# A transformer block pair on one core: the first stage's small work in another order

## The reference

```
xn   = rmsnorm(x, attn_norm_g)
proj = xn @ w_in                    # 1024 x 2312
qa, ka, va, qb, kb, vb, f = split(proj)
qa, ka, qb, kb = rmsnorm of each head (64 wide), with gains
out_a = sliding-window attention (8 query, 2 key heads, alibi, a sink logit per head)
log_f = log_sigmoid(f + b_forget)
out_b = causal attention (8 heads), logit[t, s] += c[t] - c[s], c = cumsum(log_f)
x = x + concat(out_a, out_b) @ w_out
x = x + relu(rmsnorm(x) @ w_up)**2 @ w_down
```

## Time and profile before

| | |
|---|---|
| time, three runs | 1270.38, 1275.14, 1274.62 us; median 1274.62 |
| the profiled execution's own time | 1270.3 us |
| its span, first to last instruction | 1268.4 us |
| TensorE busy | 1208.7 us, 95% of the span |
| VectorE, ScalarE, GpSimd busy | 610.9, 464.6 and 450.8 us |
| mean granted TensorE clock | 0.987 of full |
| first TensorE instruction | 10.12 us |
| tiles 0 to 3 of the first stage (first matmul of tile 0 to first of tile 4) | 14.99 to 48.52 us |
| first scores | 66.40 us |

### The profile page before, as it was taken

One profiled execution on the slowest core, in us unless ns is written; L12 is line 12 of the kernel. 1 busy time (PEld: TensorE's weight loads), 2 busy tenths in 40 slices (PEclk: granted clock), 3 DMA queues, 4 the chain that ended last, 5 costly groups with the idle time before them and its releaser, 6 DMA issues.

```text
span 1268.4 us, 16854 instructions
## 1 busy us (share of the span) xinstructions
PE 1208.7 (95%) x6252; PEld 998.0 (79%) x6252; DVE 610.9 (48%) x907; ACT 464.6 (37%) x828; POOL 450.8 (36%) x188
## 2 busy tenths in 40 slices
PE   5799999998999999999899999999899999999997
PEld 4677877787788788788779887778788888888885
DVE  5555445658767768651657223884721111111115
ACT  5455433425324334234342111432463251341441
POOL 3422220204444453463336320400255435353440
PEclk9999999999999999999889999999999999999999
DMA  7422120206665766643424311202243324233211
GB/s 228 116 85 67 62 87 2 85 17 216 233 215 191 241 211 210 227 134 132 133 67 143 99 67 26 67 2 83 67 140 108 119 67 132 67 105 94 83 50 66
DMA packets 75562, 144.10 MB, mean 114 GB/s; under 512 B 7234, under 2 KB 10050, under 8 KB 75490
## 3 DMA queue, kind: packets, MB, share of 16 engines
q1 hardware_dynamic: 53730, 98.46, 24.7%
q10 hardware_dynamic: 21760, 44.67, 10.6%
HBM read 140.20 MB, written 2.13 MB: 112 GB/s over the span
## 4 chain that ended last, share of the span: by engine, by line
PE 54%; issue 22%; DVE 11%; POOL 8%; ACT 2%; DMA 1%; ACTq 0%; POOLq 0%; DVEq 0%
PE gemm L950 16%; PE gemm L952 16%; PE gemm L951 16%; POOL w_lo L513 8%; DVE nmax L1860 1%; PE aux L1404 1%; DVE prob_t L1674 1%; DVE gemm L1859 1%; PE aux L991 1%; DVE xr L1465 1%; DVE xr L1460 1%; ACT junk L576 1%; DVE xt_lo L1471 1%; DMA mlp_gain<-in_g_pre_mlp 1%; PE gemm L1088 1%
## 5 line engine op out<-in xcount | busy, mean ns | idle before, releaser
L513 POOL TENSOR_TENSOR w_lo<-w_raw,w_hi 128x1024 fp32r<-128x1024 f32 (+1 forms) x180 | 445.7, 2498 | 780.2 <-ACT w_hi L741 422.3
L950 PE MATMUL gemm<-xt_hi,w_hi 128*128 128x512 f32 (+1 forms) x704 | 255.9, 363 | 5.0 <-issue 4.6
L951 PE MATMUL gemm<-xt_lo,w_hi 128*128 128x512 f32 (+1 forms) x704 | 254.8, 362 | 0.0
L952 PE MATMUL gemm<-xt_hi,w_lo 128*128 128x512 f32 (+1 forms) x704 | 254.5, 362 | 0.0
L950 PE MATMUL gemm<-w_hi,ht_hi 128*128 128x512 f32 x512 | 201.4, 393 | 3.8 <-POOL w_lo L513 3.8
L951 PE MATMUL gemm<-w_lo,ht_hi 128*128 128x512 f32 x512 | 200.0, 391 | 0.0
L952 PE MATMUL gemm<-w_hi,ht_lo 128*128 128x512 f32 x512 | 199.7, 390 | 0.0
L741 ACT ACTIVATE w_hi<-w_raw 128x1024 fp32r<-128x1024 f32 x124 | 125.7, 1050 | 175.6 <-PE gemm L952 130.0
L950 PEld LDWEIGHTS gemm<-xt_hi,w_hi 128*128 128x128 f32 x704 | 134.0, 190 | 27.1 <-issue 6.0
L1699 DVE TENSOR_TENSOR ht_lo<-hid,ht_hi 128x512 fp32r<-128x512 f32 x64 | 53.0, 828 | 210.7 <-ACT hid L754 210.7
L951 PEld LDWEIGHTS gemm<-xt_lo,w_hi 128*128 128x128 f32 x704 | 133.9, 190 | 20.2
(11 more groups left out here) (218 smaller groups left out, 1487.0 us busy)
## 6 DMA issues: line engine op xcount, KB each, us to landing
wm<-in_w_mod ACTq DMA_DIRECT2D x64, 512.0 KB, 4.8
w_raw<-in_w_in SPq DMA_DIRECT2D x32, 512.0 KB, 3.8
w_raw<-in_w_up SPq DMA_DIRECT2D x32, 512.0 KB, 4.0
w_raw<-in_w_down SPq DMA_DIRECT2D x32, 512.0 KB, 4.1
w_raw<-in_w_mlp_in SPq DMA_DIRECT2D x32, 512.0 KB, 4.2
w_raw<-in_w_mlp_out SPq DMA_DIRECT2D x32, 512.0 KB, 3.7
w_raw<-in_w_out SPq DMA_DIRECT2D x16, 512.0 KB, 3.7
x<-in_x SPq DMA_DIRECT2D x4, 512.0 KB, 7.7
```

What stands on the lines that cost most here:

```text
L513: pool.tensor_tensor(w_lo[s % 2][:, ks, 0:width], raw[q][:, :, 0:width], w_hi[s % 2][:, ks, 0:width].bitcast(F32), ALU.subtract).then_inc( ...
L950: pe.matmul(bank, lh, rh, start=(k == 0), stop=False)
L951: pe.matmul(bank, lh, rl, start=False, stop=False)
L952: mm = pe.matmul(bank, ll, rh, start=False, stop=(k == KT - 1))
```

## The change

Each engine's program gets another order in the first stage; nothing is computed otherwise.

- ScalarE: slab 0 is rounded in the first two of the four `stat` steps instead of the second and third. The Exp for silu and the copy to negsel leave the place ahead of the head chain, for h = 12 and h = 10.
- TensorE: `turn_heads(g - 3)` instead of `turn_heads(g - 2)` in the middle of tile g, for g = 3 to 7; the last three are at the ends of steps h = 0, 1 and 2. `forget_turns()` moves behind the products of h = 3. `scores(0)` waits for SINK_STEPS = 11 instead of SILU_STEPS = 12 of the same semaphore.
- ScalarE: `head_gain` moves with the turns, to g - 3, and to h = 0, 1 and 2 for tiles 5 to 7.
- VectorE: the sinks' nine instructions move from ahead of the head chain to behind `head_rows(3)`; silu's three to h = 13.

```diff
 # ScalarE
             for m in range(TT):
                 stat(STAT_N1 + m, (x_loaded[m], 16), x[:, m, :])
-                if m in (1, 2):
-                    high_of(0, 2 * m - 2)
-                    high_of(0, 2 * m - 1)
+                if m < 2:
+                    high_of(0, 2 * m)
+                    high_of(0, 2 * m + 1)
                 if m >= 1:
                     xt_high(NT_1 + m - 1, m - 1)
...
-            act.wait_ge(vec_loaded, 16 * 9)
-            did(act.activation(ctmp[:], cvec[:], ACT.Exp, scale=-1.0), silu_act)
-            act.wait_ge(negsel_loaded, 16)
-            did(act.activation(negsel[:], sel_raw[:], ACT.Copy), negsel_ready)
...
-                if g >= 2:
-                    head_gain(g - 2)
+                if g >= 3:
+                    head_gain(g - 3)
...
-                for g in range(6, 16):
-                    if (g - 6 if g < PHASE else tile_end(g) + 3) == h:
+                for g in range(5, 16):
+                    if (g - 5 if g < PHASE else tile_end(g) + 3) == h:
                         head_gain(g)
+                if h == 10:
+                    act.wait_ge(negsel_loaded, 16)
+                    did(act.activation(negsel[:], sel_raw[:], ACT.Copy), negsel_ready)
+                if h == 12:
+                    act.wait_ge(vec_loaded, 16 * 9)
+                    did(act.activation(ctmp[:], cvec[:], ACT.Exp, scale=-1.0), silu_act)
 # TensorE
-                if g >= 2:
-                    if g == 2:
+                if g >= 3:
+                    if g == 3:
                         pe.wait_ge(xt_lo_done, 2 * TT)
-                    turn_heads(g - 2)
+                    turn_heads(g - 3)
...
-                    pe.wait_ge(silu_step, SILU_STEPS)
+                    pe.wait_ge(silu_step, SINK_STEPS)
...
+                for g, k0, k1 in tile_groups(h):
+                    part_product(g, k0, k1)
+                if h < 3:
+                    turn_heads(5 + h)
                 if h == 3:
                     forget_turns()
-                for g, k0, k1 in tile_groups(h):
-                    part_product(g, k0, k1)
-                if h < 2:
-                    turn_heads(6 + h)
 # VectorE
-            (the three instructions of silu and the nine of the sinks, ahead of the gains)
+            def sinks():
+                dve.wait_ge(vec_loaded, 16 * 9)
+                rest = sink
+                for part in range(3):
+                    did(dve.tensor_copy(sink_parts[:, part, :], rest[:]), silu_step)
+                    if part < 2:
+                        did(dve.tensor_tensor(sink_rest[:], rest[:], sink_parts[:, part, :], ALU.subtract), silu_step)
+                    rest = sink_rest
+                did(dve.memset(sink_rows[:], 0.0), silu_step)
+                for part in range(3):
+                    did(dve.tensor_copy(sink_rows[32 * part:32 * part + 1, :], sink_parts[:, part, :]), silu_step)
+            def silu():
+                dve.wait_ge(silu_act, 1)
+                did(dve.tensor_scalar(ctmp[:], ctmp[:], 1.0, None, ALU.add), silu_step)
+                did(dve.reciprocal(csil[:], ctmp[:]), silu_step)
+                did(dve.tensor_tensor(csil[:], csil[:], cvec[:], ALU.mult), silu_step)
             for g in range(PHASE):
                 head_means(g)
                 head_rows(g)
+                if g == 3:
+                    sinks()
...
                 forget_gates(h)
+                if h == 13:
+                    silu()
```

More of the change, by code:

```diff
@@ L1482, in _ @@
             xt_low(NT_1 + 3, 3)
[L1484 to L1499, removed]
             dve.wait_ge(heads_loaded, 16 * 8)
@@ L1538, in head_rows @@
                                           hst[:, 3, :].unsqueeze(2).broadcast_to([P, NH, HD]), ALU.mult), gemm_free)
+            def sinks():
[9 more added lines that the diff above has]
+                    did(dve.tensor_copy(sink_rows[32 * part:32 * part + 1, :], sink_parts[:, part, :]), silu_step)
+                assert tally.n[silu_step.name] == SINK_STEPS
+            def silu():
[3 more added lines that the diff above has]
+                did(dve.tensor_tensor(csil[:], csil[:], cvec[:], ALU.mult), silu_step)
             for g in range(PHASE):
@@ L1925, in _ @@
             mlp(TILE_MLP2, sub, 8 * NCH, False, last_norm, fresh=True)
-SILU_STEPS = 3 + 5 + 4
+SINK_STEPS = 2 + 5 + 4
 POOL_STEPS = 1 + (1 + 2 + 3 + 4) + 2 * 4
```

## The result

The changed kernel takes 1278.91 us (median of 8 runs, 1277.82 to 1280.6), the kernel before 1274.63 us (8 runs, 1270.38 to 1275.83). The ratio is 1.0033, 95% interval 1.002 to 1.0047: 4.2 us slower. The forecast was 1280 us, +5.3.

A forecast was written before the change was run, and what follows sets the result against it. TensorE, busy 95% of the span, was taken as the bound, so its idle time counts; +3.5 - 6.3 + 3.4 + 2.3 + 2.4 = +5.3 us takes the median to 1280 us, range 1272 to 1286.

The forecast's parts named there:

- The start: Tile 0: roundings wait for loads, xr(1) loses VectorE's port to GpSimd, first product at 20.85 instead of 14.99: +3.5 us.
- Rival C: At the start, xr(1) loses the port twice: +2.4 us more, 1282.3 us; chance 0.13.
- The gap removed: Tiles 1 to 3: turning heads one tile later removes the 4.24 us gap and its half clock: -6.3 us.
- scores(0) and rows of tile 7: scores(0) waits for the later head_gain(4), +2.3 us; tile 7's rows wait for turn_heads(5), delaying values(1), +2.4 us.
- The sinks: Behind head_rows(3), two of VectorE's nine tiny instructions wait for GpSimd's slab 2 instructions: +3.4 us.
- The half clock at the start: After TensorE idles ahead of the first product, about 1.8 us run at half clock: 0.8 us in the sum.
- The Trainium skill's rule: Transposes don't bring up full clock; cold start would cost about 1.6 us by it, 0.8 by the rows.
- The sum: Whole kernel: the terms give +5.3 us, 1275.6 for the profiled execution, 1280 us for the median.
- Edits at nothing: Moving sinks, ctmp, negsel, silu and forget_turns adds no term of its own; without its cover negsel costs 1.0 us.

The follow-up runs named there:

- e6: Kernel before with only the head turns, their gains and forget_turns one tile later; sinks, silu and negsel where they were: ratio 0.9987.
- e3: Changed kernel with sinks() one tile earlier, behind head_rows(2) instead of head_rows(3): ratio 1.0013 against the kernel before.
- e2: Changed kernel with the rounding order undone, slab 0 rounded where it was before: ratio 1.0009 against the kernel before.
- e1: Kernel before with only slab 0 rounded in the first two stat steps: ratio 1.0031, +3.9 us.
- e4: Changed kernel with turn_heads(5) ahead of scores(0) instead of behind the products of h = 0: ratio 1.0014 against the kernel before.
- e5: Changed kernel with head_gain(4) right behind head_gain(3), in g = 6 instead of g = 7: ratio 1.0027 against the kernel before.
- e8: Kernel before profiled once more, no edit: ratio 0.9999, span 1273.3 us.
- e7: As e9, with silu and negsel late and the sinks behind head_rows(2): ratio 0.9954 against the kernel before.
- e10: As e9, with silu and negsel late and the sinks straight ahead of the head chain: ratio 0.9952 against the kernel before.
- e9: e6 with turn_heads(5) ahead of scores(0) and head_gain(4) in g = 6: 1267.98 us, ratio 0.9948 against the kernel before.

## Why the prediction was right, step by step

- **The start, forecast +3.5.** Undoing it gave 3.1 us, doing it alone 3.9. Every step is in the rows: roundings at 9.69 and 10.96 (forecast 9.7 and 11.2), xr(1) done at 18.9 (19.1), first product 20.55 (20.85), tile 1 begins at 27.95 (27.9). Rival C, xr(1) losing twice, didn't happen: it lost to one instruction and ran before the fourth.
- **The gap removed, forecast -6.3; scores(0) and rows of tile 7, +2.3 and +2.4.** Together -1.6, and e6 measured -1.7. Its parts were off by up to 2 us against each other: rows of tile 3 came later than forecast there (e6), while gain 4 and turn 5, each taken back in the changed kernel, gave 0.8 and 2.4.
- **The sinks, forecast +3.4.** The mechanism is the one forecast, two instructions each ending with a GpSimd instruction, and the size is in the rows: counted from the start of tile 4, the rows of tile 6 are done after 17.8 us in the first profile (66.28 less 48.52) and after 21.3 in the changed kernel's (66.93 less 45.64), 3.5 more. e3 gave back only 2.5, since the sinks aren't free at tile 2 either (rows of tile 3 end 4.4 us after tile 4 starts, 3.8 in the changed kernel's) and since tile 4 began 0.4 later in its profile. The pair e2 and e6 gave 2.8.
- **The half clock at the start, forecast 0.8.** The twelve matmuls from 20.55 to 24.32 took 3.8 us where the sum has 2.76 at full clock: 1.0. The same twelve cost 0.6 to 1.7 in the profiles of e1, e3, e4 and e5, which have the same start, so the size is within what single executions scatter.
- **The Trainium skill's rule** that transposes don't bring up the full clock ("TensorE: Matmul & The Clock Gate", Part 4). My sentence against it rested on one row at full clock, 0.40. Eight of the sixteen transposes ahead of the first product, in the first profile and in e8:

```profile
12.67 1.62 PE L991 MATMUL aux<-ident,xr 128*128 128x128 f32 x8 [0.58 <-DVE xr L1460]
```

```profile
12.66 1.97 PE L991 MATMUL aux<-ident,xr 128*128 128x128 f32 x8 [0.58 <-DVE xr L1460]
```

In the first profile the last of them already run faster, so there the clock rose when TensorE had run nothing but transposes, which the rule as stated excludes. But that is so in two of the twelve profiles (this one and e2's); in the other ten the first product began at half clock. The rule doesn't hold in every execution, and my "the rows disagree" said too much: the price of a cold start can't be taken from one row.

- **The sum.** Against the first profile, on which it was made, each step is within 0.7 us: tile 4 at -2.9 (forecast -2.8), scores(0) at +3.1 (+2.9), values(1) at +6.0 (+5.3). That the total then came to +4.3, a microsecond below the forecast and not above it, is the scatter of clock and order that e8 shows, which the prediction didn't reckon with: it took one execution of the kernel before as if all had its first stage. So the mechanisms were right, and that 1280 lies so near 1278.91 is in part luck. The prediction also held 0.5% for about the least that can be told from no change; the interval came out at some 0.14% either way, so the 4.2 us are clear of it.
- **Edits at nothing.** Confirmed by e7 and e10 against e9. None of the next waits took up the shift: against the first profile it is 6.0 us at values(1) and at values(2).

## What to carry to other kernels

Ask which engine's chain the end of a stage waits for before removing the waits of another: here TensorE's three gaps came back as one and left 1.7 us, and only when the two things it then waited for were moved as well did they become more. Put small VectorE work on two SBUF operands, or plain copies and casts, where GpSimd is idle; its own length is no measure of its cost. A chain that is ready a little earlier needn't be done earlier: in e8 0.35 us ahead became 1.5 us behind, because GpSimd's instructions then lay elsewhere. When a consumer is moved later, look for the buffer that it frees: the turn moved behind the scores held up the next rows, and behind them all maxima.

## What the runs showed that I had not expected

The same program's TensorE clock differs from one execution to the next at the same instruction: the first product of the first stage began with a matmul of 0.47 us in one profile of the kernel before and of 0.77 in another. From that, and from a VectorE chain that met GpSimd's instructions in another order, values(1) differed by 1.5 us and values(2) by 4.1 in the same kernel. A cast of eight numbers on one partition, with one SBUF operand, took 2.31 us beside GpSimd and 0.16 without it, as long a wait as that of an instruction on 128 x 1024 elements.
